# The context's steps get twice as many points beside the experts' products, the new ones between the two halves of each weight tile's matmuls

## What is computed

```python
# first block, experts (256 tokens, D = 1024, 32 experts, 2 used per token, d_ff = 512)
for e in range(32):
    hdn = silu(vt @ w_gate[e]) * (vt @ w_up[e])
    y = y + (combine[:, e:e + 1] * hdn) @ w_down[e]

# second block, layer 0 and 1, context side (hc = 256 context tokens)
uc = rms_norm_2(hc, norm_g[0]) * (1 + scale_c) + shift_c
# projections of uc; two attentions of the context over itself (8 heads each):
# gqa_sink_dense and mla_dense; gates; output projection ab_out_w
hc = hc + gate_c * yc
uc = rms_norm_2(hc, norm_g[1]) * (1 + scale_c) + shift_c
# keys and values of uc for layer 1 (c_in_w)
```

## Time and profile before

| | us |
|---|---|
| median of 3 runs | 1248.7 (1246.33 to 1248.93) |
| the profiled execution | 1248.72 |
| its span in the trace | 1246.9 |
| PE busy | 1115.9 (89%) |
| DVE busy | 475.0 (38%) |
| ACT busy | 419.4 (34%) |
| POOL busy | 223.7 (18%) |
| granted PE clock, mean | 0.977 of 2.4 GHz |
| read from memory | 331.32 MB, mean 267 GB/s |

### The profile page before, as it was taken

How to read it: one execution, slowest core, us unless ns; L and a number is a source line. 1 busy time by engine, 2 the same in 40 slices (tenths; PEclk the granted TensorE clock), 3 DMA queues, 4 the chain that set the end, 5 groups by cost and what they waited for, 6 DMA issues and landing times. The chain is left out here.

```text
span 1246.9 us, 17768 instructions
## 1 busy us (share of the span) xinstructions
PE 1115.9 (89%) x6962; PEld 726.6 (58%) x6962; DVE 475.0 (38%) x1030; ACT 419.4 (34%) x805; POOL 223.7 (18%) x327
## 2 busy tenths in 40 slices
PE   9999898899978898787788889987999899999996
PEld 7787555567532322434343425344887686999775
DVE  3568344534400101212323112005666546344554
ACT  4544344442202000103423101103335464444872
POOL 3005475100000000001211000002441223101550
PEclk9999899899989999999999999998999999999999
DMA  9656399343799999999999999996641204765300
GB/s 361 208 169 251 102 340 322 113 159 140 303 422 424 427 423 425 413 426 401 377 401 403 413 421 426 409 425 249 198 148 52 85 1 121 217 185 186 104 19 34
DMA packets 55707, 333.60 MB, mean 268 GB/s; under 512 B 5825, under 2 KB 6081, under 8 KB 43201
## 3 DMA queue, kind: packets, MB, share of 16 engines
q1 hardware_dynamic: 55616, 332.39, 69.2%
HBM read 331.32 MB, written 1.05 MB: 267 GB/s over the span
## 5 line engine op out<-in xcount | busy, mean ns | idle before, releaser
L480 ACT ACTIVATE ab<-w 128x1024 fp32r<-128x1024 f32 (+2 forms) x117 | 121.9, 1048 | 177.6 <-PE ps L496 174.2
L490 DVE TENSOR_TENSOR ab<-w,ab 128x1024 fp32r<-128x1024 f32 (+2 forms) x96 | 118.4, 1239 | 138.9 <-ACT ab L480 138.8
L2425 PE MATMUL ps<-w,vT 128*32 128x512 f32 x1024 | 128.8, 626 | 37.1 <-DMA w<-in_w_gate 20.3
L496 PE MATMUL ps<-ab,uA 128*128 128x512 f32 x320 | 103.1, 404 | 3.1 <-ACT gr L1440 1.3
L2425 PEld LDWEIGHTS ps<-w,vT 128*32 128x32 f32 x1024 | 28.7, 111 | 118.3 <-issue 60.9
L496 PE MATMUL ps<-UA,ab 128*128 128x256 f32 x512 | 93.5, 284 | 3.2 <-ACT h L1440 1.5
L496 PE MATMUL ps<-ab,UA 128*128 128x512 f32 (+1 forms) x288 | 87.9, 386 | 1.5 <-POOL UB L618 1.5
L496 PEld LDWEIGHTS ps<-UA,ab 128*128 128x128 f32 x512 | 80.2, 192 | 4.5 <-issue 1.7
L2473 PE MATMUL ps<-w,bT 128*32 128x512 f32 x512 | 63.0, 616 | 17.9 <-DMA w<-in_w_down 12.4
L490 POOL TENSOR_TENSOR ab<-w,ab 128x1024 fp32r<-128x1024 f32 (+1 forms) x21 | 50.0, 2384 | 127.8 <-ACT ab L480 127.8
L496 PE MATMUL ps<-UB,ab 128*128 128x256 f32 x256 | 72.4, 283 | 0.0
(11 more groups left out here) (542 smaller groups left out, 1976.3 us busy)
## 6 DMA issues: line engine op xcount, KB each, us to landing
w<-in_w_gate SPq DMA_DIRECT2D x32, 2048.0 KB, 13.1
w<-in_w_up SPq DMA_DIRECT2D x32, 2048.0 KB, 12.8
w<-in_w_down SPq DMA_DIRECT2D x32, 2048.0 KB, 13.1
w<-in_w_ada SPq DMA_DIRECT2D x48, 512.0 KB, 7.9
w<-in_w_c SPq DMA_DIRECT2D x42, 512.0 KB, 3.9
w<-in_w_m SPq DMA_DIRECT2D x16, 512.0 KB, 5.0
w<-in_ab_out_w SPq DMA_DIRECT2D x10, 512.0 KB, 4.6
w<-in_w_out SPq DMA_DIRECT2D x8, 512.0 KB, 5.4
```

The lines of the kernel that those rows point to most:

```text
L480: e.activation(sp.a(j), w.v, ACT.Copy).then_inc(sp.whole, 1)
L490: e.tensor_tensor(sp.b(j), w.v, sp.a(j).bitcast(F32), ALU.subtract).then_inc(sp.parts[j % NAB], 1)
L496: ins = e.matmul(out_, l[x], r[y], start=start and n == 0, stop=stop and n == 2)
L2425: ins = e.matmul(t.ps[o, :], ve[:, p % 2, 2 * c + k, o], w.v[:, 2 * a + k, :], start=c + k == 0, stop=c + k == 4)
```

## The change

Twice as many points: `go` is now also called in the middle of each piece (after k = 0 of gate and up, after c = 0 of down), and 4, 8 or 12 calls of `follow` become 8, 16 or 24. The constants of the targets are doubled with them.

```diff
-        CTX_WORK, CTX_POINTS, CTX_FROM, CTX_LAST, CTX_NORM2 = 1901, 94, 8, 81, 1552
+        CTX_WORK, CTX_POINTS, CTX_FROM, CTX_LAST, CTX_NORM2 = 1901, 188, 16, 162, 1552
...
                             ins = e.matmul(t.ps[o, :], ve[:, p % 2, 2 * c + k, o], w.v[:, 2 * a + k, :], start=c + k == 0, stop=c + k == 4)
+                        if k == 0:
+                            pace.go()
...
                         if f == 3:
                             ins.then_inc(t.full, 1)
+                        if c == 0:
+                            pace.go()
                     if f < 3:
                         ins.then_inc(down_used, 1)
...
         def act_sparse(e, steps):
             pace = Pace(steps)
             for p in range(GROUPS):
-                for _ in range(4):
+                for _ in range(8):
                     pace.follow()
```

More of the change, by code:

```diff
@@ L2601, in pool_sparse @@
                                 bc(comb[:, :, GROUP * p:GROUP * p + GROUP], 3, CAP), ALU.mult).then_inc(weighed, 1)
-                for _ in range(12):
+                for _ in range(24):
                     pace.follow()
```

## The result

The changed kernel takes 1258.8 us in the median of five runs (1251.92 to 1259.58). The kernel before, on the same chip, takes 1248.8 (1246.33 to 1250.46). The ratio is 1.0059, with a 95% interval of [1.0036, 1.0083]. I had forecast no change, 1248.0 us and at most 1253.0. One execution of a variant, 1428 us in `attention_only`, was in a slow state of the chip and is left out of its ratio.

A forecast was written before the change was run, and what follows sets the result against it. Loads were taken to bound the stage up to 583 us, PE to 717, loads again to 850. Terms -4.1 + 1.5 + 0.6 = -2.0, plus 1.3 gave -0.7: 1248.0 us from 1248.7, range 1243.5 to 1253.0.

The forecast's parts named there:

- Price of a split: Pieces with steps both in the middle and behind pay one more way in and out on PE, about 0.3 us.
- Gain in the attentions: In both attentions, halves of pieces hide behind the chain through DVE and ACT; together -4.1 us of PE's time.
- (a): At d0 of the fourth place the release comes 1.5 us later, and so does the load of d3: +1.5 us.
- (e): Other held slots release 3.6 us later but find another piece queued: counted 0, up to 1 us at each of three places.
- (b): Behind d3, PE asks for a piece every 4.8 us but loads need 4.92, so it waits for g3: +0.6 us.
- (c): PE is again the bound; at 700 us it is 2.0 us early, and the loads behind 717 us follow.
- (d): d1 of the seventh place holds its slot for the norm's 7.9 us, so g0's load comes late: +1.3 us.
- rival C: A load's data start once sent, so the norm leaves no dry queue and (d) is 0: 1246.7 us, chance 0.10.
- The clock at the end: The last two pieces ran at half clock; less idling might gain up to 1.4 us or cost more; counted 0.
- B: Releases behind middle steps come late and starve the loads: 1254 us, or 1251.5 in a milder case; chance 0.25.
- the three signs: Wrong if rate from 342 to 570 falls below 420, DMA waits appear 610-700 us, or 583-700 isn't 3-4 us shorter.

The follow-up runs named there:

- attention_only: The changed kernel with steps only in the middles of pieces 45 to 68, beside the two attentions; ratio 1.0015 [0.9994, 1.0037] to the kernel before.
- second recording: A second profiled execution of the unedited changed kernel; 1257.5 us, span 1255.7, where the first recording took 1251.92 us.
- norm_only: The kernel before, with only the second norm put in the middle of d1 of the seventh place; ratio 1.0014 [0.9998, 1.0030].
- the early tile: Each projection weight tile asked for one step earlier; 0.9982 in the kernel before, 1.0009 with the projections' middles (1.0055 without it), 1.0033 in the whole change.
- aligned_early: Middles in the attentions alone, no point ending right behind transposes t, projection tiles one step earlier; 1247.7 us, ratio 0.9973 [0.9956, 0.9991] to the kernel before.

## Why the prediction was wrong

Read at the recorded pair, where the forecast was -0.7 and the span says +3.2:

- **Price of a split: right.** From d3 of the fourth place to the `turn` of the sixth the time is 699.24 - 583.49 = 115.75 us, before 699.96 - 583.02 = 116.94. Waits for engines (the sum of all rows of PE's waits there but those for loads) fell from 18.3 to 8.6 us; those for loads rose by 2.3, the 3.1 shown less the 0.81 ahead of 583.49. So 115.75 - 116.94 + 9.7 - 2.3 = 6.2 us are left for the splits: 20 by 0.3 are 6.0.
- **Gain in the attentions: right, -3.5 for -4.1** (6.2 - 9.7). The waits went from 13 to 7.
- **(a) +1.5: the number lies between the 0.7 and 3.0 us of the two recordings, but not for the reason given.** I had PE on time at the fourth `turn`; it was 1.4 and 3.9 us late there, which belongs to (e). The piece at 583.02, which I had near 584.5, started at 583.49.
- **(b) +0.6: too small.** Loads took back 2.3 us (halves at 588.46, 594.21, 641.82 and 646.71 now wait for their pieces), since the queue was nearly full there all along: 401 of 426 GB/s. What PE gains above the rate of loads is lost at once.
- **(c) -2.0 at 700 us, and the loads behind follow: failed.** It was 699.24 - 699.96 = -0.7. And by the seventh `turn`, at 765.25 (before 764.73) it had become +0.5: another 1.2 us, in a stretch where slots are held for projection steps (g0 of the seventh place, at 718.63 behind 3.14 us, before at 717.71 behind 1.84). That piece also ran 3.62 us in place of 1.92, so hold and clock aren't separated here.
- **(d) +1.3: the mechanism right, the size wrong.** 46.51 - 43.58 = 2.9 us in this recording, 4.5 in the other. I had taken the release for 776.7, since PE should have been early by 2.0; it was 779.5, as PE was late instead. The queue also ended earlier than reckoned: 11.1 us behind the landing of d1 at 769.34 would be 780.4, but only 124 GB/s moved from 777 to 780. So rival C, without a dry queue at the norm, is out.
- **(e) held slots at projections, counted at nothing, up to 1 us at three places: this is the step that failed.** Middles at the projections alone cost 0.55%, 5.9 us by the means of the runs (1255.6 against 1249.7). In the recorded pair they are the 1.4 us at the fourth `turn`, and 3.9 in the second recording. I had argued that one more piece is always queued behind the one coming in. The rate near 425 GB/s spoke for it, and it was the wrong sign to read: it tells that the queue was never empty before, not by how much. I had also left out the clock there: the step of 3.70 us took 5.40 in the held slot, and the section on the clock looked at the last pieces only.
- **The clock at the end: put at 0.** The last stretch, from the last `turn` on, took 19.5 us in place of 20.7, which is within the -1.4 I had allowed. But `attention_only` and `norm_only`, with no middle there, have 19.3 as well, so it isn't the middle's doing.

The measured parts, -0.7, +1.2, +2.9 and -0.2 behind the norm, give the +3.2. The rival that came true is B, held slots starve the loads, at 1251.5 to 1254 for this recording (1251.9); how much of its price is the hold and how much the clock stays open. For the median it was still too cheap by about 5 us. (Its lower figure is added up wrongly: 2 + 3 + 1.5 - 4.1 is +2.4, 1251.1 us.) As to what would make me wrong, two of the three signs came: waits for loads between 610 and 700 us, and the stretch from 583 to 700 us shorter by 1.2 instead of 3 to 4. The third, a rate under 420 from 342 to 570, didn't come in the first recording (420) and came in the second (418).

The Trainium skill, page "TensorEngine Tiling (Array Packing)", Key Properties, has a change of tiling mode drain the engine. The 6.2 us for 20 splits are such a price as the rows of the kernel before already had. It wasn't this that made the loss: `attention_only` has these 20 splits and stands at 1.0015 [0.9994, 1.0037].

**What stays open.** The traces tell 2.1 us of stage for the projections' middles (491.8 for 489.7), the runs 5.9. The span of that recording is 7.2 us longer than before; 1.8 of it lie ahead of the first `turn` and 3.3 behind the stage, where single executions vary by as much. It isn't settled how the loss is shared between the longer hold itself, the steps at half the clock and the tile's wait: the three come together wherever a half waits for its piece. The runs only bound the last, loosely (0 to 0.3%). A kernel that holds the slots as long and keeps the clock up, or the reverse, would tell; none was run. The sum of the parts (0.55 projections, 0.14 norm, 0.15 attentions) is 0.84%, the whole is 0.55 to 0.59; with intervals of 0.2% each that is no contradiction, and no proof that they add.

## What to carry to other kernels

Where a queue of loads waits in order for the release of a slot, work put between the first and the last use of that slot can be paid by the loads, even if the engine has room, as the norm shows. Before moving a step there, read for each slot how much is still queued at its release: a rate near full says only that it wasn't zero. And give a fix that works its control in the kernel before: the early tile looked like the proof of a cause, and the control showed two fifths of its effect where that cause is absent.

## What the runs showed of the hardware

- An empty queue costs more than the gap in it. Behind g0, sent at 779.59, the rate from 780 to 783 us was still 240 GB/s of 426 (366 before); behind the release at 580.6, 104 GB/s from 580 to 583.
- The same projection step of eight instructions took 5.40 us right behind a half that had waited 1.26 us for its piece (granted clock 0.68), and 3.70 in the earlier trace rows. The stretch of the first place had a granted clock of 0.93 in place of 1.00 (1.2 of 2.4 GHz for part of it), and PE was busy for 40.80 instead of 37.49 us. That stretch had 0.96 in `norm_only` too, which has no middle there, so the middles aren't all that lowers it. In the kernel before it was the last two pieces that ran slower behind such waits; here it is a step twice as long.
- PE's busy time in the stage grew by 15.5 us, and in `aligned_early` by 5.6, where the stage was 4 us shorter: with loads as the bound, busy time alone tells nothing of the end.
